# Where four more weight tiles of the first expert group are put between a mixer and its experts

## The chip, the cores and the metric

The kernel runs as one program on one core of a Trainium2 chip. The metric is the device time of one execution in microseconds (us); the time of a kernel is the median over its runs. All arithmetic is float32.

## The reference, cut to what matters

Two blocks follow each other over 256 tokens of width 1024. The first block has two layers; each is a mixer (attention in two branches) and then a layer of 16 experts (the change touches the start of the latter):

```
for l in range(DEPTH):                       # DEPTH = 2
    h = h + hybrid_mixer(rmsnorm(h, norm_mix[l]), ...)
    h = h + expert_choice_ffn(rmsnorm(h, norm_ffn[l]), w_router[l],
                              w_expert_gate[l], w_expert_up[l], w_expert_down[l])
```

Each expert picks its 32 best tokens (256 tokens x 2 / 16 experts), takes them through silu(x @ gate) * (x @ up), and through down, and adds the results back, weighted by the router's probability. All three matrices are 1024 x 1024 for each of the 16 experts, 12 MiB in float32, so 192 MiB of weights pass through the core in each layer. The second block (an attention layer, a state-space layer and two retrieval layers) follows and is not touched.

## The kernel before, in words

**Order.** The time runs: mixer 0, experts 0, mixer 1, experts 1 (names `m0.`, `x0.`, `m1.`, `x1.`), then the second block (`ma`, `p0`, `b`, `p1`). Each engine has its own written-out program (`sync_program`, `tensor_program`, `vector_program`, `scalar_program`, and one for GpSimd); they meet only at semaphores. `at["name"]` is the semaphore and value at which something named is done, and `X.wait_ge(*at["name"])` waits for it. A program waits in its order: whatever stands behind a wait in the same program waits too.

**The weights' way.** SyncE (SP) issues all weight loads in one fixed order. A load takes the next of six slots of `wbuf` (128 partitions x 4096 float32, 2 MiB each), after waiting until the tile that held the slot before was read (`<tile>.used`). That is `load_parts`, whose DMA is issued at L460, and `Ring(6)`.

**Experts.** The 16 experts are done in four groups `g` of four. A group has 8 tiles of gate weights (`x{l}.g{g}.w0` to `w7`), 8 of up (`u`) and 8 of down (`d`), so 96 tiles a layer. A tile holds a 128-row chunk `c` of one matrix for the four experts. In `wide` (L847) TensorE takes the tiles in order, 16 matmul records a tile: four experts stand beside each other in the array, each with 32 picked tokens as stationary columns. `XE` holds the picked tokens, turned, for all four groups; `SI` the silu products; `AT` those turned; `YE` the result of a group; `PA`, `PG` and `PT` the one-hot matrices of the picks, the same times the router's weight, and those turned. In `experts(l, extra)` TensorE does `pick(0)`, then all of gate and up of group 0, then the picks of groups 1 to 3 and `places()` (which needs `PG`), then goes on.

**Between mixer and experts.** The mixer ends with `ya` and `yb` (the two branches' products; `MT` is their gated sum, finished part by part as `mt0` to `mt3`), and the residual with `wo0` and `wo1`. Then come the norm, the router (`rl`), the softmax and the four rounds of maxima that choose the tokens, and the picks. The last six mixer tiles in `wbuf` are `w11`, `wa`, `wb0`, `wb1`, `wo0`, `wo1`; the first six expert tiles `g0.w0` to `g0.w5` take their slots as each is read; `g0.w6` waits for `g0.w0.used`.

**The memory around it.** `ar` is an arena of 16384 float32 a partition that mixer, experts and second block lay out differently. `cbuf` holds the mixer's bias tables, `HT` the normed and turned tokens.

Of the kernel before, what the change touches and what calls it, by code (L numbers as in the profile page):

```python
# [8 lines left out]
ACT = mybir.ActivationFunctionType  # L9
# [114 lines left out]
def program(nc, I, out):  # L124
    ctx = ExitStack()
    with ctx:
# [3 lines left out]
        def sem(name):  # L130
            return ctx.enter_context(nc.semaphore(name))

        Y = sb("Y", [P, 2, 1024])
        HT = sb("HT", [P, 8, 256])
# [5 lines left out]
        cbuf = sb("cbuf", [P, 2, 1536])  # L140
        ar = sb("ar", [P, 16384])
# [7 lines left out]
        tile_landed = [sem(f"tile_landed{k}") for k in range(6)]  # L149
        rows_landed = [sem(f"rows_landed{k}") for k in range(8)]  # L150
        table_landed = [sem(f"table_landed{k}") for k in range(2)]
        landed = {n: sem(f"{n}_landed") for n in (
            "consts", "x", "router", "relin", "mem", "bias", "keys0", "keys1", "row")}
        zd_written = sem("zd_written")
        out_written = sem("out_written")

        at = Marks()
        place, shape = {}, {}

        def C(name):  # L160
            return co[:, CO[name][0]:CO[name][1]]
# [14 lines left out]
        def ps(job):  # L176
            return PS[place[job]]
# [4 lines left out]
        def arv(a, b, pat=None, **k):  # L182
            v = ar[:, a:b]
            return v if pat is None else v.rearrange(pat, **k)
# [115 lines left out]
        PA = arv(0, 1024, "p (i n) -> p i n", i=2)  # L300
        PG = arv(1024, 2048, "p (i n) -> p i n", i=2)
        PT = arv(2048, 3072, "p (g t) -> p g t", g=4)
        XE = arv(3072, 7168, "p (c n) -> p c n", c=8)
        wr = arv(7168, 7296, "p (c n) -> p c n", c=8)
        SI = arv(7296, 9344, "p (k n) -> p k n", k=2)
        AT = arv(9344, 11392, "p (k c n) -> p k c n", k=2, c=8)
        YE = arv(11392, 12416)
        af = arv(12416, 12448, "p (i n) -> p i n", i=2)
        mk = arv(12448, 12480, "p (i n) -> p i n", i=2)
        ky = arv(12480, 12512, "p (i n) -> p i n", i=2)  # L310
# [7 lines left out]
        oh = ar[0:32, 13824:14335]  # L318
        rb = small(480, 12)[0:32, :]
        gb = arv(15360, 16384)  # L320


        aQT = arv(0, 1536, "p (c t) -> p c t", c=6)
# [118 lines left out]
        def rows_of(name):  # L442

            k = place[name]
            return wbuf[:, shape["row_tiles"][k // 2], 2048 * (k % 2):2048 * (k % 2) + 2048]

        def wtile(name):
            k, nk, n = shape[name]
            return wbuf[:, k, 0:nk * n].rearrange("p (k n) -> p k n", k=nk)


        def sync_program(S):
            count, tiles = {}, Ring(6)
# [12 lines left out]
            def load_chunk(name, W, l, g, c):  # L466

                load_parts(name, I[W][l, g, c], 4, 1024)
# [43 lines left out]
                    load(f"m{l}.wo{h}", I["w_out"][l], 512 * h, 8, 512)  # L512

            def expert_tiles(l):
                def gate_up(g):
                    for n, W in (("g", "w_expert_gate"), ("u", "w_expert_up")):
                        for c in range(8):
                            load_chunk(f"x{l}.{n}{g}.w{c}", W, l, g, c)

                def down(g):  # L520
                    for c in range(8):
                        load_chunk(f"x{l}.d{g}.w{c}", "w_expert_down", l, g, c)

                for g in range(4):
                    gate_up(g)
                    if g == 1 and l:
                        S.wait_ge(*at["x1.xe3.1"])
                        S.land(S.e.dma_start(Y[:, :, :], I["mem_2"][0].rearrange("(i p) n -> p i n", p=P)),
                               landed["mem"], count, "mem.in")
                        row("row.final", "final")  # L530
                    if l and g > 1:
                        load(f"mem.w{g - 2}", I["w_mem_kv_2"][g - 2], 0, 8, 512)
                    if g:
                        down(g - 1)
                down(3)
# [8 lines left out]
            for l in range(2):  # L544
                mixer_tiles(l)
                S.wait_ge(*at[f"m{l}.win.pv7"])
                S.land(S.e.dma_start(ar[:, 7168:7296], I["w_router"][l]), landed["router"], count,
                       f"x{l}.wr")
                if l == 0:
                    S.wait_ge(*at["m0.t11.out"])  # L550
                    S.land(S.e.dma_start(oh, I["oh"]), landed["relin"], count)
                    S.land(S.e.dma_start(rb, I["rel_bias_2"]), landed["relin"], count, "rel.in")
                expert_tiles(l)
            W = I["a_w_in_2"][0]
# [47 lines left out]
        def tensor_program(T):  # L602
# [65 lines left out]
            def tile(name):  # L668
                T.wait_ge(*at[name])
                return wtile(name)  # L670
# [120 lines left out]
            def experts(l, extra):  # L791
# [46 lines left out]
                def wide(jobs, name, lhs):  # L838


                    for job in jobs:
                        take(job)
                    for c in range(8):
                        v = tile(f"{name}.w{c}")
                        for n in range(2):
                            for k in range(4):
                                m = T.e.matmul(ps(jobs[n])[32 * k:32 * k + 32, :], lhs(c, k),  # L847
                                               v[:, k, 512 * n:512 * n + 512], start=(c == 0), stop=(c == 7),
                                               tile_position=(0, 32 * k))
                        T.did(m, f"{name}.w{c}.used", *([name] if c == 7 else []))  # L850

                def gate_up(g):
                    for k in range(2):
                        T.wait_ge(*at[f"{p}xe{g}.{k}.out"])
                    for n in ("g", "u"):
                        wide([f"{p}{n}{g}.{i}" for i in range(2)], f"{p}{n}{g}",
                             lambda c, k: XE[:, c, 128 * g + 32 * k:128 * g + 32 * k + 32])

                def turn(g):
                    T.wait_ge(*at[f"{p}u{g}.1.out"])  # L860
# [336 lines left out]
        def vector_program(V):  # L1197
# [3 lines left out]
            def tt(o, a, b, op, *names):  # L1201
                V.did(V.e.tensor_tensor(o, a, b, op), *names)  # L1202
# [205 lines left out]
            def experts(l, extra):  # L1408
# [33 lines left out]
                def pick(g, k):  # L1442
                    job, g0 = f"{p}xe{g}.{k}", PF[f"norm_ffn{l}"][0] + 4 * k
                    V.wait_ge(*at[job])
                    tt(XE[:, 4 * k:4 * k + 4, 128 * g:128 * g + 128], ps(job)[:, :].rearrange("p (c n) -> p c n", c=4),
                       pf[:, g0:g0 + 4].unsqueeze(2).to_broadcast([P, 4, 128]), ALU.mult, job + ".out")

                pick(0, 0)
                pick(0, 1)
                for i in range(2):  # L1450
                    tt(PG[:, i, :].rearrange("p (e c) -> p e c", e=16), PA[:, i, :].rearrange("p (e c) -> p e c", e=16),
                       af[:, i, :].unsqueeze(2).to_broadcast([P, 16, 32]), ALU.mult, *([p + "pg"] if i else []))
# [430 lines left out]
        def scalar_program(A):  # L1883
# [5 lines left out]
            def act(o, i, f, *names, **kw):  # L1889
                A.did(A.e.activation(o, i, f, **kw), *names)  # L1890
# [141 lines left out]
            def experts(l, extra):  # L2032
                p = f"x{l}."
                norm(f"x{l}", f"norm_ffn{l}", lambda i, h: f"m{l}.r{h}{i}.out")
                m1, s1 = small(16, 2), small(18, 2)
                A.wait_ge(*at[p + "nm1"])
                for i in range(2):
                    act(af[:, i, :], ps(p + "rt")[:, 16 * i:16 * i + 16], ACT.Exp, *([p + "ex"] if i else []),
                        bias=m1[:, i:i + 1], accum_out=s1[:, i:i + 1])
                def pick(g, k):  # L2040
                    job = f"{p}xe{g}.{k}"
                    A.wait_ge(*at[job])
                    for n in range(4):
                        c = 4 * k + n
                        act(XE[:, c, 128 * g:128 * g + 128], ps(job)[:, 128 * n:128 * n + 128], ACT.Copy,
                            *([job + ".out"] if n == 3 else []), scale=gain(f"norm_ffn{l}", c))

                def gate_up(g):
                    A.wait_ge(*at[f"{p}g{g}"])
                    for n in range(2):  # L2050
                        act(SI[:, g % 2, 512 * n:512 * n + 512], ps(f"{p}g{g}.{n}")[:, :], ACT.Silu, f"{p}g{g}.{n}.out")

                def down(g):
                    A.wait_ge(*at[f"{p}d{g}"])
                    copy(YE[:, 512:1024], ps(f"{p}d{g}.1")[:, :], f"{p}d{g}.1.out")

                for g in range(4):
                    gate_up(g)
                    if g == 0:
                        for k in range(2):  # L2060
                            pick(1, k)
                        A.wait_ge(*at[p + "pt0"])
                        copy(PT[:, 0:2, :], two(ps(p + "pt0")[:, :]), p + "pt0.out")
                    next(extra, None)
                    if g:
                        down(g - 1)
                    A.wait_ge(*at[f"{p}tn{g}.0"])
                    copy(AT[:, g % 2, 0:4, :], ps(f"{p}tn{g}.0")[:, :].rearrange("p (k n) -> p k n", k=4), f"{p}tn{g}.0.out")
                down(3)
                drain(extra)  # L2070
# [476 lines left out]
```

## Time and profile before

| | |
|---|---|
| median of 3 runs | 3207.03 us (3205.33 to 3211.16) |
| the profiled execution: its time | 3205.56 us |
| its span, first to last instruction | 3203.7 us |
| TensorE busy, share of the span | 2553.3 us, 80% |
| granted TensorE clock, mean | 0.923 |
| moved by DMA | 1101.86 MB, mean 344 GB/s |

The span is 1.86 us shorter than the profiled execution's own time. TensorE's busy time counts matmuls whose ends are modelled, so it says where the engine works, not how well. The clock is given as a share of full speed: 1.00 is 2.4 GHz, 0.50 is 1.2 GHz. The DMA share is the mean busy share of the core's 16 DMA engines; it can read 1.01 where they never rest.

### The profile page before, as it was taken

The page shows a single profiled execution, that of the slowest core. Times are in us where ns is not written, and L with a number is a line of the kernel's source. Part 1 is how long each engine was busy: PE and PEld are TensorE (multiplying, and loading weights), DVE is VectorE, ACT ScalarE, POOL GpSimd, SP SyncE. Part 2 cuts the span into 40 slices and gives each one's busy share as a digit, 9 for nine tenths or more (in the row PEclk, how much of TensorE's full clock was granted, in tenths as well). Part 3 has the DMA queues.
Part 4 walks back from the last instruction along what each step waited for, and adds up shares of the span by engine and source line. Part 5 has one row for each costly group of instructions (what it writes and reads, how often), then busy time and mean ns, then how long its engine had stood idle before and what let it go on. Part 6 is the DMA issues. An engine that isn't in the chain of part 4 may idle for free.

```text
span 3203.7 us, 31231 instructions
## 1 busy us (share of the span) xinstructions
PE 2553.3 (80%) x10802; PEld 1314.0 (41%) x10802; DVE 1359.4 (42%) x3265; ACT 881.3 (28%) x2329; POOL 583.8 (18%) x557
## 2 busy tenths in 40 slices
PE   8998766656999875666598887789897989977776
PEld 6775311111777521122165642245462544523222
DVE  0352100001144200000244767777867687677774
ACT  1231000000122101000123334455633475343433
POOL 0000000000000000000001334433434344344442
PEclk9999877787999887788899999999999999999999
DMA  7324899999533299999911899999999999999997
GB/s 287 127 103 155 341 428 428 428 428 428 209 121 132 105 422 427 428 427 428 423 74 63 340 422 421 421 421 402 419 422 421 410 414 408 420 421 422 421 421 317
DMA packets 120188, 1101.86 MB, mean 344 GB/s; under 512 B 13376, under 2 KB 17248, under 8 KB 20960
## 3 DMA queue, kind: packets, MB, share of 16 engines
q1 hardware_dynamic: 44576, 559.83, 42.1%
q0 software_dynamic: 73728, 536.90, 40.4%
q10 hardware_dynamic: 1728, 3.14, 0.3%
q8 instruction: 86, 1.41, 0.2%
q14 instruction: 70, 0.57, 0.0%
HBM read 1095.64 MB, written 4.19 MB: 343 GB/s over the span
## 4 chain that ended last, share of the span: by engine, by line
PE 42%; DMA 41%; DVE 9%; ACT 4%; issue 3%; POOL 0%; SPq 0%; DVEq 0%; ACTq 0%; POOLq 0%
PE ps L619 23%; DMA wbuf<-in_puv,ar 18%; PE ps L1173 9%; DMA wbuf<-in_w_expert_up 8%; DMA wbuf<-in_w_expert_down 8%; DMA wbuf<-in_w_expert_gate 4%; PE ps L847 4%; DVE ar L1841 3%; ACT ar L1890 2%; PE ps L719 2%; PE ps L623 2%; DMA wbuf<-in_w_mem_kv 2%; PE ps L705 1%; ACT L1890 1%; DMA Y<-in_mem 1%
## 5 line engine op out<-in xcount | busy, mean ns | idle before, releaser
L1173 PE MATMUL ps<-wbuf,ar 128*128 128x512 f32 x2048 | 968.2, 611 | 217.5 <-ACT ar L1890 217.3
L1841 DVE CUSTOM_DVE_ANT_0 ar<-wbuf,Y 128x1024 f32<-128x1024 f32 x512 | 627.4, 1225 | 334.8 <-DMA wbuf<-in_puv,ar 326.0
L847 PE MATMUL ps<-wbuf,ar 128*32 128x512 f32 x3072 | 495.0, 783 | 316.1 <-DMA wbuf<-in_w_expert_up 133.7
L2367 POOL DMA_INDIRECT wbuf<-in_puv,ar x512 | 558.7, 1091 | 842.5 <-PE ps L1173 804.8
L1173 PEld LDWEIGHTS ps<-wbuf,ar 128*128 128x128 f32 x2048 | 368.2, 192 | 769.8 <-issue 768.0
L619 PE MATMUL ps<-HT,wbuf 128*128 128x256 f32 (+2 forms) x2784 | 500.1, 339 | 12.5 <-DMA wbuf<-in_w_mem_kv 4.5
L619 PEld LDWEIGHTS ps<-HT,wbuf 128*128 128x128 f32 (+1 forms) x2784 | 439.2, 192 | 71.8 <-issue 14.1
L1890 ACT ACTIVATE ar<-ar 128x1 f32<-128x1 f32 (+2 forms) x1052 | 270.1, 257 | 657.6 <-DVE ar L1841 629.8
L847 PEld LDWEIGHTS ps<-wbuf,ar 128*32 128x32 f32 x3072 | 99.4, 127 | 699.0 <-issue 205.7
L2351 POOL TENSOR_TENSOR sm<-sm,co 128x1 f32<-128x1 f32 (+1 forms) x17 | 10.7, 632 | 1689.1 <-DVE sm L1208 1355.3
L1887 ACT COPY ar<-ps 128x512 f32<-128x512 f32 (+2 forms) x131 | 72.0, 550 | 620.4 <-PE ps L847 307.2
L1199 DVE COPY ar<-ps 128x512 f32<-128x512 f32 (+4 forms) x96 | 58.4, 608 | 432.7 <-PE ps L847 274.3
L1202 DVE TENSOR_TENSOR ar<-ar,ps 128x512 f32<-128x512 f32 (+1 forms) x20 | 13.2, 661 | 532.5 <-PE ps L847 532.1
L1890 ACT ACTIVATE ar<-co,ar 128x128 f32<-128x128 f32 x512 | 205.5, 401 | 18.2 <-PE ps L1173 1.5
L1890 ACT ACT_TABLE_LOAD x105 | 134.7, 1283 | 135.1 <-PE ps L847 69.7
L619 PE MATMUL ps<-wbuf,HT 128*128 128x256 f32 (+3 forms) x464 | 130.8, 437 | 0.0
L619 PE MATMUL ps<-ar 64*128 64x256 f32 (+3 forms) x508 | 100.8, 399 | 10.0 <-DVE ar L1199 8.2
L619 PEld LDWEIGHTS ps<-wbuf,HT 128*128 128x128 f32 x464 | 85.3, 197 | 41.1 <-issue 34.2
L1890 ACT ACTIVATE ar<-ps 128x512 f32<-128x512 f32 (+2 forms) x48 | 24.0, 499 | 269.4 <-PE ps L847 189.6
L1890 ACT ACTIVATE ar<-ar,sm 128x257 f32<-128x257 f32 (+1 forms) x80 | 47.6, 595 | 175.8 <-DVE sm L1206 70.1
L619 PEld LDWEIGHTS ps<-ar 64*128 64x128 f32 (+1 forms) x508 | 56.5, 189 | 61.6 <-issue 38.3
L1202 DVE TENSOR_TENSOR X<-X,ps 128x512 f32<-128x512 f32 x56 | 38.5, 687 | 97.8 <-PE ps L719 43.1
(139 smaller groups left out, 1506.9 us busy)
## 6 DMA issues: line engine op xcount, KB each, us to landing
wbuf<-in_w_expert_gate SPq DMA_DIRECT2D x64, 2048.0 KB, 26.3
wbuf<-in_w_expert_up SPq DMA_DIRECT2D x64, 2048.0 KB, 26.2
wbuf<-in_w_expert_down SPq DMA_DIRECT2D x64, 2048.0 KB, 27.3
wbuf<-in_w_in SPq DMA_DIRECT2D x22, 2048.0 KB, 11.2
wbuf<-in_peer_w_q SPq DMA_DIRECT2D x12, 2048.0 KB
wbuf<-in_w_o SPq DMA_DIRECT2D x6, 2048.0 KB, 7.1
wbuf<-in_b_w_in SPq DMA_DIRECT2D x6, 2048.0 KB
wbuf<-in_w_branch_b SPq DMA_DIRECT2D x4, 2048.0 KB, 15.3
```

Of the source, the lines that this page charges most:

```text
L619: m = T.e.matmul(o, l, r, start=(n == 0), stop=(n == len(pairs) - 1))
L623: return T.e.transpose(o, i, ident[0:i.shape[0], 0:i.shape[0]])
L705: m = T.e.matmul(ps(job)[po:po + 64, c0:c0 + w], v, units[j]["pb"][:, a:a + w], start=start, stop=stop, tile_position=(0, po))
L719: m = T.e.matmul(b[:, :], lhs[:, c, 128 * i:128 * i + 128], v[:, c, :], start=(c == 0), stop=(c == 7))
L847: m = T.e.matmul(ps(jobs[n])[32 * k:32 * k + 32, :], lhs(c, k), v[:, k, 512 * n:512 * n + 512], start=(c == 0), stop=(c == 7), tile_positi ...
L1173: m = T.e.matmul(acc[n][:, :], DG[:, j % 4, :], rows_of(name)[:, 1024 + 512 * n:1536 + 512 * n], start=(j == 0), stop=(j == 127))
L1199: V.did(V.e.tensor_copy(o, i), *names)
L1202: V.did(V.e.tensor_tensor(o, a, b, op), *names)
L1841: V.did(V.e.tensor_tensor_reduce(JK, rows_of(f"g{l}{i}.{j}")[:, 0:1024], Y[:, i, :], 1.0, 0.0, ALU.mult, ALU.add, DT[:, i, j:j + 1]), f"do ...
L1887: A.did(A.e.copy(o, i), *names)
L1890: A.did(A.e.activation(o, i, f, **kw), *names)
L2367: G.land(G.e.indirect_dma_start(out=rows_of(name), out_offset=None, in_=I["puv"], in_offset=bass.IndirectOffsetOnAxis(ap=IX[:, i, j:j + 1] ...
```

## The change

Four of the 16 gate and up tiles of the first group go to memory outside the ring: `g0.w2`, `g0.w5`, `g0.w6` and `u0.w1`. The other 92 tiles of a layer use the six slots as before, in the same order. Each of the four has its own condition, on which SyncE waits in its place in the order, and its own semaphore. Their places are parts of `ar` that the experts fill later, `cbuf`, and `HT`. To make room, `XE` is laid out by group first, the router's weights `wr` move within the arena, and `SI`, `AT` and `YE` shift by 128. Two of the four tiles are loaded in pieces (two and three DMAs). `PG` lies in a piece of `g0.w5`'s place, so VectorE waits for `g0.w5.used` before it computes `PG`.

```
-        XE = arv(3072, 7168, "p (c n) -> p c n", c=8)
-        wr = arv(7168, 7296, "p (c n) -> p c n", c=8)
+        XE = arv(3072, 7168, "p (g c n) -> p g c n", g=4, c=8)
...
+        wr = arv(13680, 13808, "p (c n) -> p c n", c=8)
...
+        spare = [[ar[:, 4096:8192]], [cbuf[:, :, :].rearrange("p k n -> p (k n)"), ar[:, 1024:2048]],
+                 [ar[:, 8192:12288]], [HT[:, :, :].rearrange("p c t -> p (c t)"), ar[:, 2048:3072], ar[:, 14336:15360]]]
...
+                aside = {("g", 2): (0, (m + "win.pv7", m + "ya0.out")),
+                         ("g", 5): (1, (m + "cw2.used", m + "cw3.used", m + "wb1.used")),
+                         ("g", 6): (2, (m + "win.pv7", m + "mt3")),
+                         ("u", 1): (3, (f"x{l}.rl",))}
+
+                def load_spare(name, W, c, k, before):
+                    for b in before:
+                        S.wait_ge(*at[b])
+                    in_spare[name] = k
+                    a = 0
+                    for piece in spare[k]:
+                        n = piece.shape[1]
+                        S.land(S.e.dma_start(piece, I[W][l, 0, c][:, a:a + n]), spare_landed[k], count,
+                               name if a + n == 4096 else None)
+                        a += n
...
                 def gate_up(g):
                     for n, W in (("g", "w_expert_gate"), ("u", "w_expert_up")):
                         for c in range(8):
-                            load_chunk(f"x{l}.{n}{g}.w{c}", W, l, g, c)
+                            if g == 0 and (n, c) in aside:
+                                load_spare(f"x{l}.{n}{g}.w{c}", W, c, *aside[n, c])
+                            else:
+                                load_chunk(f"x{l}.{n}{g}.w{c}", W, l, g, c)
...
                     for c in range(8):
-                        v = tile(f"{name}.w{c}")
+                        T.wait_ge(*at[f"{name}.w{c}"])
                         for n in range(2):
                             for k in range(4):
+                                v = expert_rows(f"{name}.w{c}", k)
                                 m = T.e.matmul(ps(jobs[n])[32 * k:32 * k + 32, :], lhs(c, k),
-                                               v[:, k, 512 * n:512 * n + 512], start=(c == 0), stop=(c == 7),
+                                               v[:, 512 * n:512 * n + 512], start=(c == 0), stop=(c == 7),
                                                tile_position=(0, 32 * k))
...
                 pick(0, 0)
                 pick(0, 1)
+                V.wait_ge(*at[f"{p}g0.w5.used"])
                 for i in range(2):
```

`expert_rows(name, k)` returns expert `k`'s 1024 columns of a tile, from the ring or from the piece that holds them.

## Rows read from the trace of the kernel before

**Rows 1.** The page: its span and the DMA share in 40 slices.

```profile
span 3203.7 us, 31231 instructions
...
DMA  7324899999533299999911899999999999999997
```

**Rows 2.** Windows by stage: busy us of each engine (instructions), PEclk, DMA share, GB/s.

```profile
238.90:333.20 94.30, 78.28 (x295) 53.60 (x293) 23.46 (x54) 14.16 (x28) 1.09 (x2) 0.87 0.37 135
...
347.80:792.20 444.40, 279.94 (x1608) 70.85 (x1608) 26.17 (x38) 17.19 (x31) 0.00 (x0) 0.79 1.01 428
...
1024.50:1118.60 94.10, 78.91 (x301) 54.64 (x299) 23.51 (x54) 15.06 (x29) 1.09 (x2) 0.89 0.37 135
...
1133.50:1583.80 450.30, 290.62 (x1728) 93.17 (x1728) 25.97 (x42) 22.87 (x47) 1.34 (x2) 0.81 1.01 427
...
1849.00:3203.70 1354.70, 1128.66 (x3459) 536.04 (x3458) 955.79 (x2143) 625.90 (x1712) 528.62 (x485) 0.99 0.99 412
```

**Rows 3.** Waits of TensorE, 335 to 790 us: total, times, longest.

```profile
PE ps L847 <- DMA wbuf<-in_w_expert_up: 67.5, 32, 3.1
```

**Rows 4.** Timeline of experts 0, start: start us, length us, what, [idle before <-releaser].

```profile
333.25 12.22 PE L847 MATMUL ps<-wbuf,ar 128*32 128x512 f32 x112 [0.90 <-DVE ar L1202]
...
335.23 2.04 SPq L460 DMA_DIRECT2D wbuf<-in_w_expert_gate  x2
...
347.81 2.69 PE L847 MATMUL ps<-wbuf,ar 128*32 128x512 f32 x16 [2.33 <-DMA wbuf<-in_w_expert_gate]
...
363.64 1.93 PE L847 MATMUL ps<-wbuf,ar 128*32 128x512 f32 x16 [1.23 <-DMA wbuf<-in_w_expert_up]
...
383.21 3.47 PE L847 MATMUL ps<-wbuf,ar 128*32 128x512 f32 x16 [2.97 <-DMA wbuf<-in_w_expert_up]
388.11 1.92 PE L847 MATMUL ps<-wbuf,ar 128*32 128x512 f32 x16 [1.42 <-DMA wbuf<-in_w_expert_up]
```

**Rows 5.** Timeline of SyncE's queue, 250 to 310 us, issues of g0.w2 to g0.w5.

```profile
258.55 0.33 SPq L460 DMA_DIRECT2D wbuf<-in_w_expert_gate  x1
...
272.36 0.33 SPq L460 DMA_DIRECT2D wbuf<-in_w_expert_gate  x1
...
286.09 0.33 SPq L460 DMA_DIRECT2D wbuf<-in_w_expert_gate  x1
...
299.82 0.33 SPq L460 DMA_DIRECT2D wbuf<-in_w_expert_gate  x1
```

**Rows 6.** Timeline from mixer 0's end to its picks, four steps of it.

```profile
240.70 1.42 DVE L1202 TENSOR_TENSOR ar<-ps,ar 128x512 f32<-128x512 f32 x2 [5.03 <-ACT ar L1890]
...
273.16 0.69 DVE L1202 TENSOR_TENSOR ar<-ar 128x512 f32<-128x512 f32 x1
...
306.53 5.95 PE L619 MATMUL ps<-HT,ar 128*16 128x256 f32 x16 [2.09 <-ACT HT L1890]
...
333.19 1.42 DVE L1202 TENSOR_TENSOR ar<-ar 128x512 f32<-128x512 f32 x2
```

**Rows 7.** Windows of 5 and 10 us, columns as in rows 2.

```profile
275.00:280.00 5.00, 5.00 (x13) 2.20 (x12) 0.69 (x1) 0.00 (x0) 0.00 (x0) 1.00 0.81 341
280.00:285.00 5.00, 5.00 (x13) 2.17 (x12) 0.00 (x0) 0.72 (x2) 0.00 (x0) 1.00 0.00 0
...
335.00:345.00 10.00, 10.00 (x100) 3.59 (x92) 0.00 (x0) 0.00 (x0) 0.00 (x0) 1.00 0.90 347
```

**Rows 8.** Timeline, VectorE's first work after group 0's up tiles.

```profile
390.20 1.41 DVE L1202 TENSOR_TENSOR ar<-ar,ps 128x512 f32<-128x512 f32 x2 [55.59 <-PE ps L847]
```

**Rows 9.** Timeline, start of experts 1.

```profile
1118.60 12.22 PE L847 MATMUL ps<-wbuf,ar 128*32 128x512 f32 x112 [0.90 <-DVE ar L1202]
```

**Rows 10.** Timeline, last expert tile and first projection after it; the last tile of experts 1.

```profile
788.83 3.38 PE L847 MATMUL ps<-wbuf,ar 128*32 128x512 f32 x16 [2.97 <-DMA wbuf<-in_w_expert_down]
...
806.55 23.76 PE L619 MATMUL ps<-HT,wbuf 128*128 128x256 f32 x109 [1.05 <-DVE HT L1202]
```

```profile
1580.54 3.20 PE L847 MATMUL ps<-wbuf,ar 128*32 128x512 f32 x16 [3.02 <-DMA wbuf<-in_w_expert_down]
```

More of the change, by code:

```diff
@@ L151, in program @@
         table_landed = [sem(f"table_landed{k}") for k in range(2)]
+        spare_landed = [sem(f"spare_landed{k}") for k in range(4)]
         landed = {n: sem(f"{n}_landed") for n in (
@@ L157, in program @@
         at = Marks()
-        place, shape = {}, {}
+        place, shape, in_spare = {}, {}, {}
         def C(name):
@@ L302, in program @@
         PT = arv(2048, 3072, "p (g t) -> p g t", g=4)
-        XE = arv(3072, 7168, "p (c n) -> p c n", c=8)
-        wr = arv(7168, 7296, "p (c n) -> p c n", c=8)
-        SI = arv(7296, 9344, "p (k n) -> p k n", k=2)
-        AT = arv(9344, 11392, "p (k c n) -> p k c n", k=2, c=8)
-        YE = arv(11392, 12416)
+        XE = arv(3072, 7168, "p (g c n) -> p g c n", g=4, c=8)
+        SI = arv(7168, 9216, "p (k n) -> p k n", k=2)
+        AT = arv(9216, 11264, "p (k c n) -> p k c n", k=2, c=8)
+        YE = arv(11264, 12288)
+        wr = arv(13680, 13808, "p (c n) -> p c n", c=8)
         af = arv(12416, 12448, "p (i n) -> p i n", i=2)
@@ L445, in rows_of, with expert_rows @@
             return wbuf[:, shape["row_tiles"][k // 2], 2048 * (k % 2):2048 * (k % 2) + 2048]
+        def expert_rows(name, k):
+            if name not in in_spare:
+                return wtile(name)[:, k, :]
+            for piece in spare[in_spare[name]]:
+                n = piece.shape[1] // 1024
+                if k < n:
+                    return piece[:, 1024 * k:1024 * k + 1024]
+                k -= n
         def wtile(name):
@@ L514, in expert_tiles @@
             def expert_tiles(l):
+                m = f"m{l}."
+                aside = {("g", 2): (0, (m + "win.pv7", m + "ya0.out")),
[12 more added lines that the diff above has]
+                        a += n
                 def gate_up(g):
@@ L546, in sync_program @@
                 S.wait_ge(*at[f"m{l}.win.pv7"])
-                S.land(S.e.dma_start(ar[:, 7168:7296], I["w_router"][l]), landed["router"], count,
+                S.land(S.e.dma_start(ar[:, 13680:13808], I["w_router"][l]), landed["router"], count,
                        f"x{l}.wr")
@@ L856, in gate_up @@
                         wide([f"{p}{n}{g}.{i}" for i in range(2)], f"{p}{n}{g}",
-                             lambda c, k: XE[:, c, 128 * g + 32 * k:128 * g + 32 * k + 32])
+                             lambda c, k: XE[:, g, c, 32 * k:32 * k + 32])
                 def turn(g):
@@ L1444, in pick @@
                     V.wait_ge(*at[job])
-                    tt(XE[:, 4 * k:4 * k + 4, 128 * g:128 * g + 128], ps(job)[:, :].rearrange("p (c n) -> p c n", c=4),
+                    tt(XE[:, g, 4 * k:4 * k + 4, :], ps(job)[:, :].rearrange("p (c n) -> p c n", c=4),
                        pf[:, g0:g0 + 4].unsqueeze(2).to_broadcast([P, 4, 128]), ALU.mult, job + ".out")
@@ L2044, in pick @@
                         c = 4 * k + n
-                        act(XE[:, c, 128 * g:128 * g + 128], ps(job)[:, 128 * n:128 * n + 128], ACT.Copy,
+                        act(XE[:, g, c, :], ps(job)[:, 128 * n:128 * n + 128], ACT.Copy,
                             *([job + ".out"] if n == 3 else []), scale=gain(f"norm_ffn{l}", c))
```

## The prediction

> **What bounds the kernel now.** I read the page first, to see where the DMA engines work without a pause and where they rest [rows 1]. Each digit is 80.1 us of the span. Three runs of nines stand there: the experts of layer 0, those of layer 1, and the second block's retrieval. Around them lie stretches at 2 to 5 tenths, the mixers. The windows by stage put numbers to it [rows 2]. In both expert stretches the DMA share is 1.01 at 427 to 428 GB/s, while TensorE is busy for 280 of 444 us. In the 94 us before each, from the end of the windowed attention to the first expert matmul, the share is 0.37.
>
> The waits then show that TensorE in the expert stretch waits for tiles to land: 32 waits for up tiles alone come to 67.5 us [rows 3]. The timeline gives the price of a tile. Once the tiles that were already there are used up, one starts at 363.64 and the fifth after it at 388.11 [rows 4]: 24.47 / 5 = 4.89 us a tile, whatever TensorE does in it. (A tile takes TensorE 1.92 us at 2.4 GHz and 3.47 us at 1.2 GHz, both less.) So from about 335 us to the end of the experts the time is the number of tiles still to be moved, times 4.89 us, plus other transfers that don't change.
>
> How many are still to be moved is set at the first expert matmul. It starts at 333.25 and runs over 112 records, that is 7 tiles of 16, in 12.22 us, 1.75 us each [rows 4]. Six of these were waiting in the ring. The seventh is g0.w6, which SyncE could issue only at 335.23, after g0.w0 was read. It landed during the run, and g0.w7 let TensorE go on at 347.81. Layer 1 shows the same 112 records in the same 12.22 us [rows 9].
>
> **The change part by part.** *Four tiles leave the stream.* In each layer, of 96 tiles, 90 are moved after the first matmul now; afterwards 86 would be, if all four new ones fit into the pause before. The pause: the stretch of 94.3 us moves at 135 GB/s against 428 when full [rows 2]. That is about 0.37 of it in use, so 59 us of DMA time are free, and four tiles need 4 x 4.89 = 19.6 us.
>
> *When each can go.* SyncE's order is g0.w0, w1, then w2 to w7, u0.w0, w1, w2. Now g0.w2 to w5 are issued at 258.55, 272.36, 286.09 and 299.82, each as a mixer tile is read [rows 5]. Afterwards:
> - g0.w2 needs ya0.out, VectorE's first product, done by 242.1 [rows 6]. It follows g0.w1, before 258.55.
> - g0.w3 and w4 take the slots freed at 258.55 and 272.36.
> - g0.w5 waits for the same wb1.used as w4, 272.4. The tables that it overwrites were used before.
> - g0.w6 needs mt3, done at 273.16 + 0.69 = 273.9 [rows 6].
> - g0.w7 and u0.w0 take the slots freed at 286.09 and 299.82.
> - u0.w1 needs the router's product, 306.53 + 5.95 = 312.5 [rows 6].
>
> None of these waits is later than the one after it in SyncE's order, so none holds up a slot that is free. The tightest knot is w4, w5, w6 from 272.4 on: three tiles, 14.7 us, to 287.1, with w7 to 292.0. Even u0.w1, from 312.5, has 20.7 us until the first matmul, and it is the tenth tile, needed only at 333.25 + 9 x 1.75 = 349.0. Two tiles in pieces add three DMA issues a layer to a queue whose issues take 0.33 us [rows 5]: 1 us in the pause, nothing on the path.
>
> *The restart.* u0.w2, w3, w4 ... now take the place that g0.w6, w7, u0.w0 ... had. The first is issued at g0.w0.used again, 335.23, since the first matmul doesn't move. The k-th tile after the restart lands when the k-th does now. But slots come free more slowly, since spare tiles are read between ring tiles. At 1.75 us a tile g0.w0, w1, w3, w4, w7 and u0.w0 are read by 335.0, 336.8, 340.3, 342.0, 347.3 and 349.0. The stream needs the third of them by about 335.2 + 2 x 4.89 = 345.0, the fifth by 354.8, the sixth by 359.7. The least margin is 4.7 us; no pause comes.
>
> *What TensorE then does.* It has ten tiles without a wait, 17.5 us, to 350.8. u0.w2 and w3 have landed by then (the second after the restart landed at 347.81), and u0.w4, due at 347.81 + 4.89 = 352.7, before TensorE comes to it at 354.3. From u0.w5 on, it waits for a tile every 4.89 us as now. u0.w7 is the sixth after the restart, where it now is the tenth. So group 0's up ends 4 x 4.89 = 19.6 us earlier, near 370.5 rather than 390.0. All that follows in the ring keeps its order and its six slots and comes 19.6 us earlier.
>
> *VectorE's new wait.* PG is now computed at 333.19 (two instructions, 1.42 us) [rows 6]. Afterwards it waits for g0.w5.used, 333.25 + 6 x 1.75 = 343.8, and is done at 345.2. Behind it in VectorE's program stands the product of group 0's silu with up, for which VectorE now sits idle 55.59 us until 390.20 [rows 8], afterwards until about 370.6. The places on TensorE need PG only after the picks. So cost nothing; the cover is 25 us. Without it, each us of lateness would be one of TensorE's, but not of the stream's until the ring's six slots (29 us) had filled.
>
> *The moved memory.* XE by group, wr elsewhere, SI, AT and YE shifted: the same instructions with the same elements, and XE's writes become contiguous. VectorE's write of a half of XE takes 0.69 us within the routing chain. I take nothing for it. If it changed by 0.1 us in each of the two writes before the first matmul, it would be 0.4 us over both layers.
>
> *Is the gain passed on?* Experts 0 end with the landing of the last down tile at 788.83; the next projection starts at 806.55 after norm and transposes, released by VectorE, not by a weight tile [rows 10]. So the load order behind the experts is ahead of need, and shifts along with them. Experts 1 end likewise on a tile at 1580.54 [rows 10]. The second block is a chain of its own after that, at share 0.99 in its long part [rows 2], and nothing in it has a fixed date.
>
> *The sum.* 2 layers x 4 tiles x 4.89 us = 39.1 us. The last tile of each expert stretch runs at either clock level, 1.92 or 3.47 us [rows 4], and the phase may shift: +-1.6 us each, +-3 us in all. Against the profiled execution: 3205.56 - 39.1 = 3166.5; it lies 1.47 us under the median of the runs, so for the median 3207.03 - 39.1 = 3167.9 us, 1.2% faster.
>
> One figure stands against this price. HBM Reference of the Trainium skill (Specifications) gives an effective 358 GB/s per core, though it says under the same heading that a core streaming alone measures well above it. This stream runs at 428 [rows 2]. By the page's share a tile would take an estimated 5.86 us and the change would bring 46.9 us; by the rows it is 4.89 us and 39.1, and the rows decide.
>
> **The rivals.** *Low clock over the backlog.* Ahead of the first expert matmul the clock is low in places (mean 0.87 in the stretch [rows 2]). If TensorE took the ten tiles at 1.2 GHz, 3.47 us each, g0.w0 would be read 1.7 us later, w3 at 347.1 and w7 at 361.0 instead of 340.3 and 347.3. The stream, restarted at 336.9, would want the first of these at 346.7 and the second at 356.9, and pause for 0.4 and 4.1 us. Together 6.2 us a layer: 39.1 - 12.4 = 26.7, 3180.3 us. Against it: the clock is 1.00 from 335 to 345 [rows 7], and 12.22 us for seven tiles in both layers [rows 4, 9]; the backlog only makes TensorE's work denser. 4 in 100.
>
> *One tile isn't hidden.* If u0.w1, issued last and in three pieces, or the knot at 272 us came too late for use, a tile of 4.89 us a layer is lost: 3207.0 - 29.4 = 3177.7. It would have to take 36.5 us from its issue at 312.5 to its use at 349.0. 4 in 100.
>
> *The gain is given back or isn't all passed on.* The stream's shift could be taken up where something else ends last: the moves of the relative tables in experts 0, or the start of the second block. For one layer's whole gain that gives 3187.5 us. Against it: the waits for tiles run to the last tile in both [rows 10]. 5 in 100. For all of it, that is the change moves tiles and no time, 3207 us: 2 in 100.
>
> *Slower: the new loads hold up the engines that work beside them.* Four tiles of 2 MiB a layer now arrive in memory that lies beside what TensorE, VectorE and ScalarE read in the same 94 us. To end slower than before, every new load would have to stop the mixer's end or the routing for longer than its own 4.89 us. If it did for 1.5 times that, 3207.0 - 39.1 + 58.7 = 3226.6 us. Against it: with the DMA engines at 0.81 and at 0.00, TensorE does 13 matmuls of the residual in 5 us [rows 7]. 2 in 100.
>
> **How the numbers follow.** The forecast, all eight tiles hidden, has 83 in 100, and its own range is 3167.9 -3.9 / +4.1: 3164 to 3172 (the phase of the last tiles and the spread of medians, as the three runs lie 2 to 4 us around theirs). The range given, 3162 to 3178, takes in the rival of the lost tile and 2 us more below; what it leaves out, the other rivals, has 13 in 100. A change under 0.2%, 6.4 us, can't be told from none here. Faster by more: the forecast and the rivals at 3180, 3178 and 3187, 83 + 4 + 4 + 5 = 96 in 100; same 2; slower 2.
>
> **What would show each step.** The DMA share before experts 0 should rise from 0.37 to 0.37 + 19.6 / 94.3 = 0.58, with no change in when the first expert matmul starts (333.25 in layer 0). The run that it begins should be 13 tiles long without a wait, 208 records in 22.7 us. SyncE's first issue after it, for an up tile, should be at 335.2 as now. The expert stretches should stay at share 1.01 and 428 GB/s. The second silu product should come near 370.6, the last tile of experts 0 near 769, the first projection of mixer 1 near 787, the last tile of experts 1 near 1541. Everything after keeps its length.
>
> The prediction is wrong if the tile rate falls with a different mix of destinations, if the first expert matmul moves, or if the stream shows a pause between 335 and 370 us.

## The result and the profile after

The changed kernel takes 3166.6 us (median of 4 runs, 3165.22 to 3167.99) against 3206.4 us before: a ratio of 0.9875, 95% interval 0.9862 to 0.9889, so 39.8 us or 1.25% faster. The forecast was 3167.9 us, in a range of 3162 to 3178.

The page of the kernel after, its span and the DMA share in 40 slices of 79.1 us, beside [rows 1]:

```profile
span 3163.4 us, 31239 instructions
...
DMA  7326899999434599999811999999999999999997
```

The slices with the stretches between mixer and experts have risen, the fourth from 4 to 6 and the fourteenth from 2 to 5. The windows by stage of the kernel after, columns as in [rows 2]:

```profile
238.90:333.20 94.30, 78.22 (x312) 51.90 (x315) 23.45 (x53) 12.68 (x27) 1.09 (x2) 0.89 0.57 221
333.20:355.00 21.80, 20.16 (x188) 7.04 (x180) 1.38 (x2) 2.48 (x3) 0.00 (x0) 1.00 0.97 401
355.00:772.60 417.60, 261.22 (x1520) 68.81 (x1520) 28.44 (x42) 15.29 (x29) 0.00 (x0) 0.80 1.01 428
...
1004.80:1099.00 94.20, 78.26 (x304) 52.72 (x306) 23.44 (x53) 12.61 (x27) 1.09 (x2) 0.87 0.56 219
...
1121.00:1543.70 422.70, 269.88 (x1632) 91.25 (x1632) 26.25 (x43) 20.70 (x45) 1.39 (x2) 0.83 1.01 427
```

The stretch before the experts now moves at share 0.57 and 0.56 instead of 0.37 twice [rows 2]. The first of these windows has the bounds of the kernel before; from the first product of `ya` to the first expert matmul of this kernel, 236.0 to 330.8, the share is 0.58. In it VectorE is busy for 23.45 us and ScalarE for 15.38, as before the change (23.46 and 15.38 in 237.5 to 333.2), and TensorE for 78.76 instead of 79.68. The stream after it still runs at 427 to 428 GB/s without a pause, only for a shorter time. SyncE's queue shows when each new load went out, where [rows 5] had only the ring's:

```profile
243.63 0.43 SPq L543 DMA_DIRECT2D ar<-in_w_expert_gate  x1
257.05 14.14 SPq L475 DMA_DIRECT2D wbuf<-in_w_expert_gate  x2
271.23 0.43 SPq L543 DMA_DIRECT2D cbuf<-in_w_expert_gate  x1
271.71 1.10 SPq L543 DMA_DIRECT2D ar<-in_w_expert_gate  x2
284.60 0.33 SPq L475 DMA_DIRECT2D wbuf<-in_w_expert_gate  x1
298.33 0.33 SPq L475 DMA_DIRECT2D wbuf<-in_w_expert_up  x1
311.49 0.33 SPq L543 DMA_DIRECT2D HT<-in_w_expert_up  x1
...
332.81 14.06 SPq L475 DMA_DIRECT2D wbuf<-in_w_expert_up  x6
```

L543 issues the four tiles outside the ring. None stands in the way of a ring tile: the ring's go out at 257.05, 270.86 (the second of the merged row), 284.60 and 298.33, each 1.5 us before its time in [rows 5], as the work on `ya` is too (236.08 instead of 237.57). The timeline of TensorE in experts 0, where [rows 4] stopped after seven tiles:

```profile
330.84 3.64 PE L883 MATMUL ps<-wbuf,ar 128*32 128x512 f32 x32 [0.90 <-DVE ar L1238]
...
348.00 5.36 PE L883 MATMUL ps<-wbuf,ar 128*32 128x512 f32 x48
356.21 1.92 PE L883 MATMUL ps<-wbuf,ar 128*32 128x512 f32 x16 [2.85 <-DMA wbuf<-in_w_expert_up]
361.11 2.87 PE L883 MATMUL ps<-wbuf,ar 128*32 128x512 f32 x16 [2.97 <-DMA wbuf<-in_w_expert_up]
366.00 3.27 PE L883 MATMUL ps<-wbuf,ar 128*32 128x512 f32 x16 [2.02 <-DMA wbuf<-in_w_expert_up]
```

From 330.84 to 353.36 it works through 13 tiles without a wait; from the fourteenth on, it again gets one every 4.89 us. Three such rows are left of the group's stream, where the kernel before had nine. The end of experts 0 and the projection after it, the thirteenth tile of experts 1 (its first matmul is at 1097.37), and its last tile:

```profile
766.65 1.92 PE L883 MATMUL ps<-wbuf,ar 128*32 128x512 f32 x16 [1.53 <-DMA wbuf<-in_w_expert_down]
...
782.84 2.40 PE L654 MATMUL ps<-HT,wbuf 128*128 128x256 f32 x10 [1.06 <-DVE HT L1238]
...
1118.38 1.92 PE L883 MATMUL ps<-wbuf,ar 128*32 128x512 f32 x16 [0.20 <-DMA wbuf<-in_w_expert_up]
...
1539.78 3.47 PE L883 MATMUL ps<-wbuf,ar 128*32 128x512 f32 x16 [2.97 <-DMA wbuf<-in_w_expert_down]
```

**Where the time went.** The start times of marked steps cut the span into pieces. They are those of the timelines, and for `ya` (its first matmul) that of the chain of work that ended last. The stream is counted from the first expert matmul to the last down tile's:

| stage | before, us | after, us | change |
|---|---|---|---|
| to the first projection of mixer 0 | 18.48 | 18.54 | +0.06 |
| mixer 0 to `ya` | 219.09 | 217.54 | -1.55 |
| `ya` to first expert matmul | 95.68 | 94.76 | -0.92 |
| **experts 0, stream** | 455.58 | 435.81 | **-19.77** |
| last tile to mixer 1's projection | 17.72 | 16.19 | -1.53 |
| mixer 1 to `ya` | 217.54 | 219.06 | +1.52 |
| `ya` to first expert matmul | 94.51 | 95.47 | +0.96 |
| **experts 1, stream** | 461.94 | 442.41 | **-19.53** |
| last tile to second block's projection | 20.37 | 20.67 | +0.30 |
| second block | 1602.79 | 1602.95 | +0.16 |
| span | 3203.70 | 3163.40 | -40.30 |

The two streams give 39.3 of the 40.3 us. The rest is scattered over untouched stages, has both signs and comes to 1.0 us. The experiments below show such scatter in kernels that differ in nothing there: the second block alone took 1598.9 us in E1 and 1603.9 us in E3.

### The profile page after: what moved, and what is told of

It reads as the page before. It is cut to its first block, busy times and chain, and to the rows that moved or that the text cites. A ratio compares the mean times of both kernels' runs of the same rounds, so it can differ in the third digit from the quotient of the medians.

```text
span 3163.4 us, 31239 instructions
## 1 busy us (share of the span) xinstructions
PE 2529.0 (80%) x10802; PEld 1312.3 (41%) x10802; DVE 1359.4 (43%) x3265; ACT 881.3 (28%) x2329; POOL 580.4 (18%) x557
## 4 chain that ended last, share of the span: by engine, by line
PE 44%; DMA 39%; DVE 9%; ACT 4%; issue 3%; POOL 0%; SPq 0%; DVEq 0%; ACTq 0%; POOLq 0%
PE ps L654 24%; DMA wbuf<-in_puv,ar 18%; PE ps L1209 10%; DMA wbuf<-in_w_expert_up 8%; DMA wbuf<-in_w_expert_down 7%; PE ps L883 4%; DMA wbuf<-in_w_expert_gate 3%; DVE ar L1878 3%; ACT ar L1927 2%; PE ps L658 2%; PE ps L754 2%; DMA wbuf<-in_w_mem_kv 2%; PE ps L740 1%; ACT L1927 1%; DMA Y<-in_mem 1%
## 5 line engine op out<-in xcount | busy, mean ns | idle before, releaser
L883 PE MATMUL ps<-wbuf,ar 128*32 128x512 f32 x2944 | 458.2, 759 | 299.0 <-DMA wbuf<-in_w_expert_up 117.2
```

## The experiments

Each experiment is an edit of the changed kernel. E1 to E4 were timed together beside the kernel before (3205.8 us there); E5 to E7 likewise (3206.9 us). Stream lengths are from the first expert matmul to the last down tile, as in the table above.

### E1: the layout and the wait alone

```
-                aside = {("g", 2): (0, (m + "win.pv7", m + "ya0.out")),
-                         ("g", 5): (1, (m + "cw2.used", m + "cw3.used", m + "wb1.used")),
-                         ("g", 6): (2, (m + "win.pv7", m + "mt3")),
-                         ("u", 1): (3, (f"x{l}.rl",))}
+                aside = {}
```

> The new memory layout and VectorE's wait before PG, but no tile outside the ring. If the gain is the four tiles taken out of the stream: as before, 3206 us within 4 us, first expert matmul run of 112 records. If a part of the gain is the layout (XE written contiguously) or the wait costs something: off by that part, and it would show in the time from the first expert matmul to the first projection of mixer 1 (473.3 us before, 452.0 changed).

Measured: 3204.4 us, ratio 0.9999 (0.9989 to 1.0009). The timeline of TensorE in experts 0:

```profile
331.18 12.22 PE L880 MATMUL ps<-wbuf,ar 128*32 128x512 f32 x112 [0.90 <-DVE ar L1235]
...
786.54 1.92 PE L880 MATMUL ps<-wbuf,ar 128*32 128x512 f32 x16 [1.48 <-DMA wbuf<-in_w_expert_down]
```

The run of 112 records in 12.22 us is back, and the stream is 786.54 - 331.18 = 455.36 us, against 455.58 before; experts 1 461.98 against 461.94. So the new layout and VectorE's wait cost and bring nothing that could be seen: 0.2 us and less in the streams, about 0.1% either way in the whole. The mark named in the expectation, first expert matmul to mixer 1's projection, is 471.7 us against 473.3; the difference lies behind the stream, in a way out of 16.30 us instead of 17.72, which the kernels below show in both lengths as well. The profiled execution was a short one, 7.5 us under that of the kernel before; 3.9 us of these lie in the second block.

### E2: two tiles a layer

```
+                aside = {("g", 2): (0, (m + "win.pv7", m + "ya0.out")),
+                         ("g", 6): (2, (m + "win.pv7", m + "mt3"))}
```

> Two tiles a layer outside the ring (g0.w2 and g0.w6), the other two in it. If each tile moved into the pause is worth its 4.89 us: half the gain, 3206.4 - 19.6 = 3186.8 us, within 3 us. If the gain came from depth past some point, or only from the tile issued last (u0.w1): nearly nothing, above 3195, or nearly all, below 3176.

Measured: 3181.9 us, ratio 0.9918 (0.9902 to 0.9935); half of the gain would be 0.9938, just outside the interval. The median lies 5 us under the expected 3186.8, where 3 were allowed. It is clearly neither nothing nor nearly all of the gain, though, and the stages are sharper:

```profile
332.72 3.64 PE L881 MATMUL ps<-wbuf,ar 128*32 128x512 f32 x32 [0.90 <-DVE ar L1236]
...
778.29 3.62 PE L881 MATMUL ps<-wbuf,ar 128*32 128x512 f32 x16 [2.97 <-DMA wbuf<-in_w_expert_down]
```

That is 445.57 us, 10.0 less than before, and 452.03 in experts 1, 9.9 less: 5.0 us a tile. The profiled run itself took 3188.1 us; the other three were at 3180 to 3182. Why these are lower than the stages ask isn't shown; the kernel before spread from 3198.7 to 3210.7 us over the 19 runs beside it, so the median of four runs can lie a few us off.

### E3: four tiles in layer 0 only

```
+                aside = aside if l == 0 else {}
```

> All four tiles outside the ring in layer 0, none in layer 1. If each layer's stream carries its own gain: 3206.4 - 19.6 = 3186.8 us, within 3 us, with experts 1 at 482 us from first expert matmul to the second block's first projection, as before, and experts 0 near 452 us to mixer 1. If the gain of layer 0 is taken up in mixer 1 or later: above 3195.

Measured: 3184.6 us, ratio 0.9929 (0.9912 to 0.9946). The stream of experts 0 is 435.91 us, of experts 1 462.05 us: the first as in the changed kernel, the second as in the kernel before. From the first expert matmul to mixer 1's projection experts 0 take 452.1 us, as expected. Experts 1 take 484.1 us to the second block's projection where 482 was expected: the way out behind their last tile took 22.04 us instead of 20.37, at a mean granted clock of 0.58 instead of 0.68. The median is 21.2 us under the kernel before, so what layer 0 gains isn't taken up later, and layer 1 needs its own tiles for its own gain.

### E4: outside the ring, but not in the pause

```
+                aside = {("u", 2): (2, (m + "win.pv7", m + "mt3", f"x{l}.g0.w0.used")),
+                         ("u", 3): (1, (m + "cw2.used", m + "cw3.used", m + "wb1.used")),
+                         ("u", 4): (3, (f"x{l}.rl",))}
...
-                V.wait_ge(*at[f"{p}g0.w5.used"])
+                V.wait_ge(*at[f"{p}u0.w3.used"])
```

> Three up tiles (u0.w2, w3, w4) lie outside the ring, but are loaded only once g0.w0 was read, so the pause before the experts carries the same six tiles as in the kernel before. If the gain is transfers moved into the pause: none, 3206 us within 4. If more room for tiles is what helps, whenever they are loaded: three quarters of the gain, near 3177.

Measured: 3205.4 us, ratio 0.9997 (0.9987 to 1.0007); streams 455.56 and 462.47 us. TensorE and the window before the experts read as in the kernel before:

```profile
331.53 12.22 PE L882 MATMUL ps<-wbuf,ar 128*32 128x512 f32 x112 [0.90 <-DVE ar L1237]
```

```profile
237.10:331.50 94.40, 78.38 (x300) 53.25 (x300) 23.44 (x53) 15.38 (x29) 1.10 (x2) 0.89 0.37 135
```

This tells the two readings of the change apart. Three places more, filled once the stream runs, brought nothing. It isn't the depth of the buffer that pays here, but transfers that leave the full stretch for the one at share 0.37.

### E5: SyncE held up at the router

```
-                         ("u", 1): (3, (f"x{l}.rl",))}
+                         ("g", 3): (3, (f"x{l}.rl",))}
```

> As the changed kernel, but the place that waits for the router's product holds g0.w3 instead of u0.w1, so SyncE stands at that wait from g0.w2 on, and seven of the ten tiles go out only from about 311.5 us. By the count of the stream: 93 tiles from 311.5 in place of 86 from 332.8, (93 - 86) x 4.89 - 21.3 = 13 us more a layer, 3166.6 + 26 = 3192.6 us, within 4. If the order of SyncE's waits doesn't matter because the pause is long enough: 3167.

Measured: 3189.9 us, ratio 0.995 (0.9934 to 0.9967), and 27.4 us above the changed kernel timed beside it (3162.5). SyncE's queue and the windows:

```profile
245.11 0.43 SPq L543 DMA_DIRECT2D ar<-in_w_expert_gate  x1
312.99 0.33 SPq L543 DMA_DIRECT2D HT<-in_w_expert_gate  x1
...
317.23 36.86 SPq L475 DMA_DIRECT2D wbuf<-in_w_expert_up  x8
```

```profile
243.60:311.50 67.90, 63.10 (x226) 40.61 (x225) 12.25 (x22) 7.55 (x19) 1.09 (x2) 0.96 0.19 75
311.50:332.30 20.80, 9.57 (x49) 7.51 (x47) 9.31 (x29) 2.01 (x5) 0.00 (x0) 0.65 0.89 357
332.30:360.00 27.70, 21.05 (x176) 6.34 (x176) 1.38 (x2) 2.48 (x3) 0.00 (x0) 0.94 1.01 426
```

After g0.w2 nothing goes out for 68 us, though four ring slots come free in that time. The streams are 449.36 and 454.45 us, 13.6 and 12.0 us more than in the first profiled execution of the changed kernel, where the count of transfers gave 13. So with as many tiles in the same four places, only 17 us are left of the 44 that the changed kernel gains in this series, because the latest condition stands early in SyncE's order. Against the kernel before there is still a gain, as the 20.8 us after the router run at share 0.89.

### E6 and E7: a quarter tile more, and the changed kernel again

```
+                                if (n, c) == ("u", 1):
+                                    S.wait_ge(*at[m + "wa.used"])
+                                    S.land(S.e.dma_start(ar[:, 15360:16384], I[W][l, 0, 2][:, 3072:4096]),
+                                           spare_landed[4], count, f"x{l}.u0.w2.rest")
+                            elif g == 0 and (n, c) == ("u", 2):
+                                load_parts(f"x{l}.u0.w2", I[W][l, 0, 2][:, 0:3072], 3, 1024)
```

> As the changed kernel, and a quarter of u0.w2 (one expert's 1024 columns) also goes ahead, into the last 1024 columns of the arena, in a sixth DMA of the pause. By the price of a tile: 2 x 4.89 / 4 = 2.4 us less than the changed kernel, 3164.2 us, about what five rounds can tell. If the first landing after the restart is set by its latency and not by its bytes, the gain is less than 1 us.

E7 is the changed kernel without an edit:

> The changed kernel once more, beside the one with a quarter tile more: 3166.6 us within 2, the yardstick for that one.

Measured: 3162.5 us with the quarter tile (3161.5 to 3167.3) and 3162.5 without (3159.0 to 3167.9). The first was expected at 3164.2, the second at 3166.6 within 2, which it missed by 4 us. By the medians nothing can be told of the quarter tile. The ratio of E7 to the kernel before, 0.9867 (0.985 to 0.9883), agrees with that of the first series. The stages show where the quarter tile's gain is and where it is hidden. First the last tile of experts 0 and what follows in E6, then in E7:

```profile
764.79 3.64 PE L893 MATMUL ps<-wbuf,ar 128*32 128x512 f32 x16 [1.73 <-DMA wbuf<-in_w_expert_down]
769.31 6.05 PE L662 MATMUL ps<-ar 128*128 128x512 f32 x8 [0.88 <-DVE ar L1245]
...
785.16 5.20 PE L662 MATMUL ps<-HT,wbuf 128*128 128x256 f32 x23 [1.05 <-DVE HT L1248]
```

```profile
766.55 1.92 PE L883 MATMUL ps<-wbuf,ar 128*32 128x512 f32 x16 [1.66 <-DMA wbuf<-in_w_expert_down]
769.36 3.70 PE L654 MATMUL ps<-ar 128*128 128x512 f32 x8 [0.88 <-DVE ar L1235]
...
782.74 7.58 PE L654 MATMUL ps<-HT,wbuf 128*128 128x256 f32 x34 [1.06 <-ACT HT L1927]
```

The streams are 434.71 against 436.06 us and 441.42 against 442.48: 1.35 and 1.06 us less, where a quarter of 4.89 is 1.22. Against the first execution of the changed kernel (435.81 and 442.41) it is 1.10 and 0.99. Both sums, 2.4 and 2.1 us, lie at the price by bytes and over the 1 us that the expectation allowed for a fixed latency; each rests on single executions. But in this execution E6 went through its last tile and the eight matmuls of the result at 3.64 and 6.05 us instead of 1.92 and 3.70, so its way to the next projection is 20.37 us instead of 16.19. The windows over that way say why (E6, then E7; PEclk is the third number from the end):

```profile
764.80:785.20 20.40, 13.37 (x41) 6.31 (x41) 6.54 (x13) 7.86 (x19) 1.35 (x2) 0.61 1.00 423
```

```profile
766.50:782.70 16.20, 9.15 (x40) 5.13 (x40) 6.53 (x13) 7.85 (x19) 1.34 (x2) 0.89 1.01 428
```

TensorE is busy for 13.37 instead of 9.15 us with the same work, 4.2 us more, at a mean granted clock of 0.61 against 0.89. That is as much as this way is longer, and more than the 2.4 us sought.

## Why the prediction was right

- **What bounds.** That the experts' time is the number of tiles left to move times 4.89 us stands: E2, E3 and the changed kernel give 5.0, 4.9 and 4.9 us for each tile moved into the pause (for the changed kernel (19.77 + 19.53) / 8 = 4.91), and E4, with three tiles outside the ring but none of them loaded in the pause, gives none.
- **When each load can go.** The forecast order of issue held, and the times to half a microsecond once the 1.5 us are taken off by which layer 0's mixer ended earlier. For u0.w1, 312.5 was said and it went out at 311.49, which is half a microsecond late by that count, as the router's product took 6.42 us instead of 5.95. The share came out at 0.57 or 0.58, by the window, where 0.58 was worked out. E5 shows that the order mattered: one late condition placed early costs 27 us.
- **The restart.** SyncE's first up tile came 1.97 us after the first expert matmul (332.81 and 330.84), as before (335.23 and 333.25 [rows 4]). There was no pause after it: share 0.97 from 333.2 to 355, which includes the restart, and 1.01 then. 13 tiles ran without a wait, as said, in 22.5 us. In layer 1 it was 12, and the thirteenth, u0.w4, waited 0.20 us. Its landing had been read from layer 0 alone, 19.45 us after the first expert matmul (352.70 - 333.25 in the timeline before). In layer 1 the third tile after the restart came 20.42 us after it before the change and 21.01 us in the changed kernel. So the cover of this step was thinner than the prediction had it.
- **VectorE's wait.** PG was computed at 341.47, where 333.19 was before; VectorE's next work, the silu product, started at 369.45, after 26.56 us of idle time:

```profile
341.47 1.42 DVE L1238 TENSOR_TENSOR ar<-ar 128x512 f32<-128x512 f32 x2 [10.73 <-PE ps L883]
369.45 1.41 DVE L1238 TENSOR_TENSOR ar<-ar,ps 128x512 f32<-128x512 f32 x2 [26.56 <-PE ps L883]
```

  E1 prices layout and wait together at nothing measurable.
- **No clock loss over the backlog.** The rival of a low clock needed 3.47 us a tile; the window 333.2 to 355 has a clock of 1.00.
- **No slowing of the work beside the loads.** From `ya` to the first expert matmul layer 0 takes 94.76 and 94.73 us with the new loads (the changed kernel, E7) and 95.68 and 94.17 us without (before, E1). The slower rival needed over 19 us there.
- **What was off.** The prediction had named a move of the first expert matmul as a sign of being wrong, and it came at 330.84 instead of 333.25. The moved tiles needn't be the cause: 1.55 us lie in mixer 0 before `ya` and 0.92 us behind it, and the same matmul came at 331.18 and 331.53 in E1 and E4, which load no tile more in the pause. The marks behind it were 1 to 4 us early by this and by the shorter way out: last tile of experts 0 at 766.65 (769 forecast), first projection of mixer 1 at 782.84 (787), last tile of experts 1 at 1539.78 (1541).
- **What was luck.** The sum was for the tiles alone, and the streams measured 39.3 for 39.1 us; this is the part that is right by its mechanism. That the whole came within 1.3 us of the forecast is in part luck, as the second series of the same kernel (E7) came 4.1 us lower. The forecast's own range allowed about 4 us for the phase of the last tiles and the spread of medians; the table shows more places for such scatter. It may not be scatter alone: every kernel with tiles moved into the pause gained more in the whole than in its two profiled streams, from 0.5 us (the changed kernel) over 1.7 (E3), 3.0 (E6), 3.3 (E5) and 4.1 (E2) to 5.4 us (E7), where E4 and E1 gained 1.0 and 1.3 more. What this rest is isn't shown.

The figure of 358 GB/s per core, which HBM Reference of the Trainium skill (Specifications) gives as the share of a core, would have given an estimated 46.9 us. The stream ran at 427 to 428 GB/s after the change too, and the gain was 39.3 us in the streams. The rows were the right price for this program, which runs on one core; what a tile costs beside a second core that streams, no run here shows.

## What to carry to other kernels

Where a stretch is bound by transfers and the one before it is not, count the bytes that could go earlier, and look for any memory that is dead between the two, in as many pieces as it comes; here each tile moved was worth its transfer time (4.9 to 5.0 us for 4.89), while three places more inside the full stretch were worth nothing. Order such loads in the issuing queue by when their memory becomes free, as one late condition holds up all that stand behind it (27.4 us in E5). When a step's worth is under the scatter of whole runs, read it from the stage that it acts on, between two marks of the timeline.

## What the runs showed of the hardware

- **The same mixer comes in different lengths.** From its first projection to `ya`, a mixer took either 217.5 us (mixer 1 before; mixer 0 after; both of E7 to 0.01 us) or 219.1 us (mixer 0 before; mixer 1 after; both of E1). In mixer 0 the difference between before and after lies where TensorE's mean granted clock was 0.83 between 140 and 150 us before, and 1.00 after:

```profile
140.00:150.00 10.00, 8.11 (x37) 4.97 (x36) 4.57 (x13) 2.34 (x5) 0.00 (x0) 0.83 0.66 259
```

```profile
140.00:150.00 10.00, 7.61 (x43) 4.87 (x42) 4.88 (x13) 2.57 (x5) 0.00 (x0) 1.00 0.65 249
```

  In mixer 1 it is the other way round: after, the clock is 0.83 from 902.84 to 912.84, and before it is 1.00 at the same place of the mixer (926.55 to 936.55). What makes it fall there isn't shown. It isn't the only such place: mixer 0 took 219.1 and 219.5 us in E4 and E5, with a clock of 1.00 in this stretch. There the first ten matmuls of the mixer took 3.87 and 4.28 us instead of 2.23, although the clock reads 1.00 for them too.
- **The way out of a transfer-bound stretch depends on the clock that TensorE happens to have there.** From the last down tile to mixer 1's projection it took 16.19, 17.72 and 20.37 us in three kernels (after, before, E6) with the same instructions, at a mean granted clock of 0.89, 0.71 and 0.61, with TensorE busy for 9.17, 10.73 and 13.37 us. A gain that ends in such a place can be blurred by 4 us in a single execution.
- **Loads from HBM into memory that lies between operands in use cost these nothing that shows:** mixer end and routing took 94.2 to 95.7 us at share 0.37 (before, E1) and 94.7 to 95.5 us at 0.56 to 0.58 (after, E7).
